# A feed-forward way down in seven products of half blocks, for sixteen of its twenty-two weight tiles

## The reference

```python
def conv_ffn(h, buf, w_up, b_up, w_dw, b_dw, w_down, b_down):
    u = h @ w_up + b_up                       # 1024 -> 5632
    xp = jnp.concatenate([buf.astype(u.dtype), u], axis=1)
    new_buf = xp[:, xp.shape[1] - (FFN_K - 1):]
    c = causal_dwconv(xp, w_dw, b_dw)         # 3 taps
    a, v = jnp.split(c, 2, axis=-1)
    return (jax.nn.silu(a) * v) @ w_down + b_down, new_buf   # 2816 -> 1024
...
        x = x + out
```

## Time and profile before

| | us |
|---|---|
| median of 3 runs (2735.18 to 2738.17) | 2737.77 |
| the profiled execution | 2733.82 |
| its span, first to last instruction | 2732.0 |
| PE busy | 2674.6 (98%) |
| DVE busy | 2121.9 (78%) |
| POOL busy | 1283.9 (47%) |
| ACT busy | 842.9 (31%) |
| mean DMA rate | 86 GB/s |

### The profile page before, as it was taken

The page is one execution under the profiler, slowest core; times in us unless marked ns, Lnnn a source line. Parts: engine busy times, 40 slices in busy tenths (PEclk is TensorE's granted clock), DMA queues, the critical chain, the costliest instruction groups (busy, mean ns, idle before and its releaser), DMA issues.

```text
span 2732.0 us, 42103 instructions
## 1 busy us (share of the span) xinstructions
PE 2674.6 (98%) x17516; PEld 2631.1 (96%) x17516; DVE 2121.9 (78%) x2447; ACT 842.9 (31%) x1267; POOL 1283.9 (47%) x928
## 2 busy tenths in 40 slices
PE   8999989999999999999999999999999999999998
PEld 8999889999999999999999999989999999999998
DVE  8998657999999855566777777797799999985555
ACT  3001624444444300021221221232444444430002
POOL 5223484777777522252212122127577777752224
PEclk9999999999999999999999999999999999999999
DMA  5222143222221432231111111115322222243222
GB/s 157 55 63 52 57 185 132 73 73 73 73 73 73 177 106 81 91 116 47 40 48 48 40 48 42 46 57 191 132 73 73 73 73 73 73 176 105 84 91 78
DMA packets 136398, 233.78 MB, mean 86 GB/s; under 512 B 67984, under 2 KB 86416, under 8 KB 136208
## 3 DMA queue, kind: packets, MB, share of 16 engines
q1 hardware_dynamic: 59120, 137.12, 14.7%
q10 hardware_dynamic: 77088, 93.97, 10.2%
HBM read 171.86 MB, written 59.20 MB: 85 GB/s over the span
## 4 chain that ended last, share of the span: by engine, by line
PE 86%; DVE 9%; POOL 3%; issue 1%; ACT 1%; DMA 0%; ACTq 0%; DVEq 0%; POOLq 0%
PE BANKS L1066 34%; PE BANKS L1026 26%; PE BANKS L1355 13%; PE BANKS L1629 3%; PE BANKS L1173 2%; PE BANKS L1411 2%; PE BANKS L1399 1%; PE BANKS L1314 1%; DVE C L2716 1%; POOL WL L828 1%; DVE XL L2302 1%; DVE HGA L2874 1%; PE BANKS L1456 1%; PE BANKS L1466 1%; DVE BANKS L2390 0%
## 5 line engine op out<-in xcount | busy, mean ns | idle before, releaser
L1066 PE MATMUL BANKS<-XB_A,OPS 128*128 128x288 f32 x3432 | 513.1, 298 | 7.9 <-ACT U L1996 7.8
L825 POOL TENSOR_TENSOR SMALL<-WRAW 128x1 f32<-128x1 f32 x108 | 26.8, 248 | 1005.4 <-PE BANKS L1026 502.2
L1066 PEld LDWEIGHTS BANKS<-XB_A,OPS 128*128 128x128 f32 x3432 | 475.1, 189 | 12.3 <-issue 10.1
L1066 PE MATMUL BANKS<-XB_B,OPS 128*128 128x288 f32 x2904 | 436.2, 295 | 0.0
L1026 PE MATMUL BANKS<-GHL,WH 128*128 128x384 f32 x2100 | 421.7, 335 | 6.3 <-POOL WL L828 3.6
L1066 PEld LDWEIGHTS BANKS<-XB_B,OPS 128*128 128x128 f32 x2904 | 403.5, 189 | 0.0
L1026 PEld LDWEIGHTS BANKS<-GHL,WH 128*128 128x128 f32 x2100 | 369.6, 188 | 7.7 <-issue 4.0
L2529 DVE TENSOR_TENSOR X<-BANKS,X 128x1152 f32<-128x1152 f32 x152 | 206.2, 1357 | 218.3 <-PE BANKS L1026 210.9
L2716 DVE SCALAR_TENSOR_TENSOR C<-U,HGA,C 128x1168 f32<-128x1168 f32 x176 | 275.8, 1587 | 40.9 <-ACT C L2015 39.4
L828 POOL TENSOR_TENSOR WL<-WRAW,WH 128x1024 fp32r<-128x1024 f32 x108 | 264.7, 2451 | 8.6
L855 POOL TENSOR_TENSOR OPS<-RAW,OPS 128x512 fp32r<-128x512 f32 x126 | 164.0, 1314 | 199.0 <-ACT OPS L1924 199.0
(11 more groups left out here) (308 smaller groups left out, 5033.3 us busy)
## 6 DMA issues: line engine op xcount, KB each, us to landing
WRAW<-in_w SPq DMA_DIRECT2D x100, 512.0 KB, 3.5
RAW<-in_w SPq DMA_DIRECT2D x84, 512.0 KB, 4.3
GR<-g_kept ACTq DMA_DIRECT2D x22, 1152.0 KB, 5.3
g_kept<-C ACTq DMA_DIRECT2D x44, 512.0 KB, 2.6
x_kept<-X ACTq DMA_DIRECT2D x24, 576.0 KB, 3.1
XB_BF<-x_kept SPq DMA_DIRECT2D x16, 576.0 KB, 8.0
ops_kept<-PRE SPq DMA_DIRECT2D x14, 512.0 KB, 2.6
OPS<-ops_kept SPq DMA_DIRECT2D x14, 512.0 KB, 3.7
```

The source lines that it names most:

```text
L1066: ins = nc.tensor.matmul(out[:, cols], w[:, a, p, :], x[:, b, cols], start=s in OPENS and p == 0 and q == 0, stop=p == PAIRS - 1 and q == ...
```

## The change

In both layers the way down keeps three groups as they are: 0, 1 and 10 (PLAIN), that is the first four and the last two weight tiles. The sixteen tiles between are taken as four quads of four tiles. A quad has two couples: a couple is the four tiles of the quad for four of the eight output tiles. It is computed in seven products of half blocks, as on the way up, for each of two pairs of output channels (ab = 0, 1), and the two pairs alternate: 14 products a couple, each 2 pairs x 3 parts x 2 pieces = 12 matmuls of 288 columns (`way_couple`). Eight couples a layer, 16 in all. "Rank" is the place of a product in its couple, 0 to 13.

- PE: product r waits for its weights (op_lo), and for DVE's read of the product four before it (read_v); each pair has two PSUM banks.
- Weights: SP loads the raw weights of a couple (four DMAs of 256 KB, rows of 1 KB) into WRAW, one buffer, after POOL's last low of the couple before. POOL makes 8 sums and 14 lows of 256 columns a couple (`way_ops`), ACT 14 highs (`way_cast`). They stand in a ring of 12 slots: four in the place of XH, eight in WH and WL. A cast waits for the product 12 before it, in couple 0 for the plain group 1.
- Inputs: SP loads the gates of a quad (eight DMAs of 288 KB) into buffers of their own for even and odd quads, each after the quad before the last. DVE makes 8 sums and 14 lows of 576 columns a quad (`way_prep`), ACT 14 highs (`way_high`), placed among the casts of the couples one ahead. DVE does one preparation of the next quad after each read from rank 5 of the first couple to rank 12 of the second, the preparations for quad 0 in groups 0 and 1, none in the last two couples.
- Output: DVE adds every product (576 columns) to half a tile of X (`way_read`), 14 a couple, in place of eight adds of 1152 a group.
- The splits of the sixteen tiles, their gates' loads on ACT's queue, high parts of 2304 columns and DVE's low parts go. The low part of group 1 goes from DVE to POOL. The last group's gates come by SP to GR_END, its low part is made by DVE in two halves in couple 7.
- The counts of the semaphores on the way up change with it (`done_no`, `read_no`, `raw_landed`), not its work. Two semaphores now serve two of the fetched parts of X each.

The core of the diff:

```diff
-FFN_UNITS = FT
-FFN_TILES = FGROUPS * KD
+PLAIN = (0, 1, FGROUPS - 1)
+QUADS = (FT - 2 * len(PLAIN)) // 4
+COUPLES = QUADS * KD // 4
+UP_ROWS = FT + 2 * COUPLES
+FFN_UNITS = 2 * len(PLAIN)
+FFN_TILES = len(PLAIN) * KD
...
+        WAY_RING = 12
...
+        WAY_PREP = (("sum", T1), ("low", B11), ("sum", NT2), ("sum", NT3), ("sum", T4), ("low", B21), ("low", NT2),
+                    ("low", T1), ("low", NT3), ("low", B22), ("low", T4))
...
+        def way_op(r):
+            slot = r % WAY_RING
+            if slot < 4:
+                v = XB_B[:, WAY_RING_AT + 512 * slot:WAY_RING_AT + 512 * (slot + 1)]
+            else:
+                of = WH if slot % 4 < 2 else WL
+                v = of[:, (slot - 4) // 4, slot % 2 * 512:(slot % 2 + 1) * 512]
+            return v.rearrange("p (h k c) -> p h k c", h=2, k=2)
...
+                def way_raw_load(n, ab):
+                    half, a = n % 2, ab * 512
+                    two = WRAW[:, ab, :].rearrange("p (a j w) -> p j a w", a=2, j=2)
+                    for j in range(2):
+                        stored = down_stored(layer, 4 * (n // 2 + 1) + 2 * j + half)
+                        sp.dma_start(two[:, j], d_w[stored, :, a:a + 512].rearrange("p (a w) -> p a w", a=2)
+                                     ).then_inc(up_raw[ab], 16)
...
+                for n in range(1, COUPLES):
+                    if n % 2:
+                        q = n // 2 + 1
+                        if q == 1:
+                            full(sp, t0 + 2 * KD - 1)
+                            sp.wait_ge(g_lo, len(PLAIN) * layer + 2)
+                        else:
+                            sp.wait_ge(up_done, way_done_no(layer, 2 * q - 3, T4, 1))
+                        if q < QUADS:
+                            for p in range(2):
+                                for s in WAY_GATE:
+                                    gate_load(q, p, s)
+                        else:
+                            sp.wait_ge(g_kept, 32 * FT * (layer + 1))
+                            sp.dma_start(GR_END[:], GKEPT[layer, FT - 2:FT].rearrange("g p t -> p g t")).then_inc(g_in, 16)
+                    sp.wait_ge(op_lo, way_op_no(layer, n - 1, T4, 1))
+                    way_raw_load(n, 0)
+                    way_raw_load(n, 1)
+                sp.wait_ge(op_lo, way_op_no(layer, COUPLES - 1, T4, 1))
+                down_load(4)
+                down_load(5)
...
+                pool.wait_ge(g_hi, layer * len(PLAIN) + 2)
+                nc.gpsimd.tensor_tensor(GHL[1][:, 1], GR[:], GHL[1][:, 0].bitcast(F32), ALU.subtract).then_inc(g_lo, 1)
+                split(u0 + 2)
+                split(u0 + 3)
+                pool.wait_ge(ffn_out, 16 * (layer + 1))
+                for n in range(COUPLES):
+                    way_ops(layer, n)
+                split(u0 + 4, used=(way_done_no(layer, COUPLES - 1, NT2, 1), up_done))
+                split(u0 + 5, used=(way_done_no(layer, COUPLES - 1, NT3, 1), up_done))
...
+                    out, a, b, how = ((0, way_raw(ab, 1, 0), way_raw(ab, 1, 1), ALU.add),
+                                      (1, way_raw(ab, 0, 0), way_tmp(ab, 0), ALU.subtract),
+                                      (0, way_raw(ab, 0, 1), way_tmp(ab, 1), ALU.add),
+                                      (1, way_raw(ab, 1, 0), way_raw(ab, 0, 0), ALU.subtract))[t]
+                    nc.gpsimd.tensor_tensor(way_tmp(ab, out), a, b, how).then_inc(op_sum, 1)
...
+                    w = way_op(way_rank(n, s, ab))
+                    pool.wait_ge(op_hi, way_op_no(layer, n, s, ab))
+                    nc.gpsimd.tensor_tensor(w[:, 1], source, w[:, 0].bitcast(F32), ALU.subtract).then_inc(op_lo, 1)
...
+                for ab in range(2):
+                    pool.wait_ge(up_raw[ab], way_raw_landed(layer, n, ab))
+                    added(ab, 0)
+                    added(ab, 1)
+                for s in (B11, B21, NT2, T1):
+                    lower(s, 0)
+                    lower(s, 1)
...
+                for ab in range(2):
+                    added(ab, 2)
+                    added(ab, 3)
+                for s in (NT3, B22, T4):
+                    lower(s, 0)
+                    lower(s, 1)
...
+                def way_couple(q, n):
+                    for s in range(PRODUCTS):
+                        for ab in range(2):
+                            pe.wait_ge(op_lo, way_op_no(layer, n, s, ab))
...
+                                pe.wait_ge(read_v, way_read_no(layer, n, s - 2, ab))
+                            w, out = way_op(way_rank(n, s, ab)), way_region(n, s, ab)
+                            for p in range(2):
+                                if n % 2 == 0 and ab == 0:
+                                    pe.wait_ge(xb_lo, way_low_no(layer, q, s, p))
+                                x = way_x(q, s, p)
+                                for k, (a, b) in enumerate(((0, 0), (0, 1), (1, 0))):
+                                    for c in range(2):
+                                        cols = slice(c * SUB, (c + 1) * SUB)
+                                        ins = nc.tensor.matmul(out[:, cols], w[:, a, p, :], x[:, b, cols],
+                                                               start=s in OPENS and p == 0 and k == 0,
+                                                               stop=p == 1 and k == 2, skip_group_check=True)
+                            ins.then_inc(up_done, 1)
...
+                def way_high(q, p, k):
+                    s = WAY_HIGHS[k]
+                    if s in (B11, B21, B22):
+                        act.wait_ge(way_in[p], 64 * (QUADS * layer + q + 1))
+                    else:
+                        act.wait_ge(xb_sum, way_sum_no(layer, q, s, p))
+                    A(way_x(q, s, p)[:, 0, :], way_whole(q, s, p), ACT.Identity).then_inc(xb_hi, 1)
+                def way_cast(n, s, ab):
+                    r = way_rank(n, s, ab)
+                    if r >= WAY_RING:
+                        act.wait_ge(up_done, way_done_no(layer, 0, 0, 0) + r - WAY_RING)
+                    elif r < 4:
+                        act.wait_ge(g_rdy, FT * (layer + 1))
+                    else:
+                        full(act, t0 + KD + (3 if r < 8 else 7))
+                    if s in (B11, B21, T4):
+                        act.wait_ge(up_raw[ab], way_raw_landed(layer, n, ab))
+                        source = way_raw(ab, 1, 1) if s == T4 else way_raw(ab, 0, s)
+                    else:
+                        t, out = {T1: (0, 0), NT2: (1, 1), B22: (2, 0), NT3: (3, 1)}[s]
+                        act.wait_ge(op_sum, way_opsum_no(layer, n, ab, t))
+                        source = way_tmp(ab, out)
+                    A(way_op(r)[:, 0], source, ACT.Copy).then_inc(op_hi, 1)
+                def way_casts(n, q, p, after):
+                    for s in range(PRODUCTS):
+                        for ab in range(2):
+                            if q < QUADS:
+                                for k in range(PRODUCTS):
+                                    if after[k] == 2 * s + ab:
+                                        way_high(q, p, k)
+                            way_cast(n, s, ab)
...
+                for k in range(PRODUCTS):
+                    way_high(0, 0, k)
+                way_casts(0, 0, 1, (0, 0, 0, 1, 2, 4, 6))
+                for n in range(1, COUPLES):
+                    q = (n + 1) // 2
+                    if n % 2:
+                        way_casts(n, q, 0, (3, 3, 4, 5, 6, 8, 10))
+                    else:
+                        way_casts(n, q, 1, (0, 0, 1, 2, 4, 6, 8))
+                gates_high(2)
...
+                def way_prep(q, p, k):
+                    what, s = WAY_PREP[k]
+                    out = way_whole(q, s, p)
+                    if what == "low":
+                        dve.wait_ge(xb_hi, way_high_no(layer, q, s, p))
+                        V.tensor_tensor(way_x(q, s, p)[:, 1, :], out, way_x(q, s, p)[:, 0, :].bitcast(F32), ALU.subtract
+                                        ).then_inc(xb_lo, 1)
+                        return
...
+                def way_read(n, s, ab):
+                    dve.wait_ge(up_done, way_done_no(layer, n, s, ab))
+                    if s in (B21, NT3, B22):
+                        dve.wait_ge(read_v, way_read_no(layer, n, {B21: B11, NT3: T1, B22: NT2}[s], ab))
+                    m = 4 * (n % 2) + 2 * ab + (s in (T1, NT3, T4))
+                    x = half(m, 0 if s in (B11, B21, T4) else 1)
+                    V.tensor_tensor(x, way_region(n, s, ab), x, ALU.add).then_inc(read_v, 1)
...
+                for n in range(COUPLES):
+                    q = n // 2 + 1
+                    for s in range(PRODUCTS):
+                        for ab in range(2):
+                            way_read(n, s, ab)
+                            at = way_rank(n % 2, s, ab)
+                            if q < QUADS:
+                                if 0 <= at - 5 < len(WAY_PREP):
```

(59 more changed lines are left out.)

184 lines of the change are left out of this document (136 added, 48 removed).

## The result

The changed kernel takes **2745.64 us** (median of ten runs, 2739.69 to 2749.53) beside 2736.09 for the kernel before (ten runs, 2734.96 to 2738.17): a ratio of 1.0033, 95% interval 1.0023 to 1.0043. It is slower by 9.6 us where 24 us less were forecast. The profiled run took 2745.89 us with a span of 2744.1, against 2733.8 and 2732.0.

A forecast was written before the change was run, and what follows sets the result against it. TensorE was taken to bound the way down. From the profiled 2733.8 us, minus 41.0 for matmuls, plus 14 for stalls and 1 for entries gave 2707.8; with 4.0 back to the median, 2712 us, range 2693 to 2735.

The forecast's parts named there:

- Part 1: Way-down matmuls: a couple takes 22.40 us, 2.56 less than a group; 16 couples in two layers save 41.0 us.
- case B: Rival, 2732 us: products of 12 matmuls cost 0.08 us each at the switch (18 us) over a stall of 17; chance 0.14.
- Part 2: GpSimd in the couples: 22 operations at 0.724 us, 15.9, plus raw load 3.8: 19.7 us a couple, 2.7 below TensorE.
- part 4: GpSimd's lead in the couples: 7.7 us at couple 1, falling 2.3 a couple; TensorE stalls 7 us a layer, 14 in all.
- Part 3: Gate preparations on VectorE beside GpSimd: blocking 0.45 us each, 5.0 for 11; a GpSimd couple 24.7 us against TensorE's 22.4.
- near 193: Sign of a right forecast: a layer's way down near 193 us for eight couples instead of 199.7.
- Part 4's own sign of failure: In the couples: the lead estimate is wrong if TensorE never waits, or waits from couple 1 on.
- Part 5: Ends of the way down: preparations and group 1's low fit into group 0; 1 us for both entries together (0 to 4).
- C: Rival, 2747 us: raw buffer's round trip, load 5 us, blocking 0.6, stalls and lower clock 56 against 41; chance 0.10.
- A: Rival, 2697 us: the cover holds in the couples, a GpSimd couple is 22.8 us, the lead lasts to the end; chance 0.28.
- the Trainium skill's rule of the whole instruction: VectorE with two SBUF inputs and GpSimd reading SBUF block each other fully; all 66 preparations paying whole length gives near 2724.

The follow-up runs named there:

- e10_entry_bare: Changed kernel with group 1's low back on VectorE and the first quad's 22 preparations writing a constant without reading: 2732.2 us, ratio 0.9990 to the kernel before.
- e9_spread: Changed kernel with group 1's low on VectorE, highs ahead of casts, T4's parts earlier, and the first quad's preparations spread over groups 0 and 1: 2699.1 us, ratio 0.9869.
- e3: Changed kernel with ScalarE making the next quad's highs ahead of the casts that wait for the raw load: 2720.6 us, ratio 0.9942 to the kernel before.
- e4: Changed kernel with T4's parts made ahead of those of NT3 and B22, so the raw load can start four GpSimd operations earlier: 2714.0 us, ratio 0.9916.

## Why the prediction was wrong

**Right.** Part 1: the pitch and the 41.0 us. Nothing stands between products of twelve, so case B's switch does not exist. Part 2: GpSimd alone takes 0.73 to 0.74 us for 256 columns against an estimate of 0.724. In the first half of a quad the stall is at the rank that part 4 names, 11; in the second half, where it names none, it is at 13.

**Part 3: the mean was right, the course was not.** GpSimd lost 145 x (0.935 - 0.729) = 29.9 us over 66 preparations between 1000 and 1170: 0.45 each, as taken. Its couples average 25.5 us against 24.7 forecast; the load is the difference, 32.6 us of waits in seven couples or 4.7 each instead of 3.8. Two things were missed. VectorE pays as well, 0.95 instead of 0.74 us for a preparation, 0.21 x 66 = 14 us a layer that the sum does not hold. And the loss is lumpy: 28 us in the couple that runs beside VectorE's dense stretch, 23 in the next. Elsewhere two numbers of the prediction are misread or slipped, and nothing rests on them: the earlier trace rows shows ScalarE busy 2.1 and GpSimd 10.7 of the 40 us, not 4 and 13, and the sum of part 4 makes eight couples 186.2 us, not the "near 193" of its signs.

**Part 4 is the step that failed.** The lead at couple 1 was to be 7.7 us. GpSimd's first low for it ended at about 1010.0 (half of a pair of 1.97 from 1009.03) and TensorE came at 1016.4: 6.4. It was to fall by 2.3 a couple, to 5.4. It fell by 5.6 (28.0 - 22.4) and more: the first low of couple 2 came at about 1038.2, and TensorE at full pitch would have come at 1038.8, a lead of 0.6. The working said itself how much lead the order wants, 4.4 us and 2.5 more in the second half of a quad, so it was gone in the first couple after the entry and not in the fourth. From there on GpSimd's whole excess is paid, 18.5 and 17.9 us in the two layers, where I had taken 7. The bound of 20 for both layers was too low as well: it let the lead shorten every layer's bill, though nearly the whole of it is needed for the order to run at all. Part 4's own sign of failure, TensorE waiting from couple 1 on, is what the trace shows.

**Part 5 failed too.** I took 1 us for both entries and 4 at most; they cost 14.6. The words "fit into the 25 us of group 0" counted GpSimd's time and not what it stands next to: the earlier trace rows had shown an operation of 1168 columns and one of GpSimd lengthen each other, and I used that row for the couples only. The preparations were added tile by tile against 3.12 us without the operations of the last way-up unit that VectorE still has to do in group 0 (one of 1168 columns and one of 1024 took 5.90 and 3.36 us beside GpSimd, 1.43 and 1.22 without). e10_entry_bare shows the two causes to be the whole of it but 0.9 us, and e9_spread that placing them otherwise is enough.

**Rivals.** C (2747 us, given one chance in ten) names the mechanism: raw round trip, meetings, lower clock. Its load of 5 us is near the 4.7, its 0.6 for a meeting is above the 0.45, and its 28 us a layer (21 of stall and 7 of clock) compare with 18 (in the window of 180 us, 9.7 and about 5). It left the entries' 14.6 out, and the two errors nearly cancel: that its 2747 is so near the measured 2745.6 is luck, though its mechanism is not. A's argument was the way up, where GpSimd works 37.3 of 50 us and TensorE loses nothing; in the couples it works 140 of 180, hardly a larger share. The meetings are there on the way up as well (L849 has a median of 1.80 us over a least of 1.29). So neither the busy share nor the meetings tell the two stages apart. In the couples it is the refill of the single raw buffer with the order behind it (e3, e4); no run tested what keeps the way up free of stalls. By the Trainium skill's rule of the whole instruction (SBUF — State Buffer, "Who interferes with whom") the prediction said 2724. That number has no working. In the prediction's own terms the rule gives a GpSimd couple of 15.9 + 3.8 + 11 x 0.75 = 28.0 us, more than C's 27.5, so C's 2747 or more. What both engines pay here for one preparation is 0.45 + 0.21 = 0.66 us of the rule's 0.75, so the rule is nearly right in size as a mean; it does not tell of the order that turns the loss into a stall.

## What to carry to other kernels

Where a producer refills a single buffer once a turn and has a few us of lead, don't spread its excess evenly over the turns: take the worst turn, and subtract from the lead what the consumers' orders need. Two engines that held each other up did no harm here once the order around them left no one waiting behind them; moving the last read of a single buffer four operations forward was worth 32 us, and moving the first quad's preparations by a few tiles 6 us by the ratios and 10 by the stages. When an operation is moved "into free time" of an engine, look up what runs beside it on the engine that it meets, not only how long it is.

## What the runs showed of the hardware

VectorE with two SBUF operands and GpSimd fall into step and stay there for eight operations of GpSimd and more, in one of two patterns: VectorE loses 0.59 us on each preparation (0.74 to 1.33) and GpSimd 0.24 on each operation (0.74 to 0.98), or VectorE loses nothing and GpSimd 0.61 (0.74 to 1.35), one operation for every add and preparation. So a preparation costs both engines together 0.59 + 2 x 0.24 = 1.07 us in the first pattern, more than its own 0.74, and 0.61 in the second; the mean of 0.66 above hides this, and some preparations meet nothing. The first pattern stood while GpSimd made the lows of four products in a row and gave way to the second where it went over to its next sums, at 1018, 1069 and 1120 us in layer 0 of the changed kernel. With reductions of the same length in the place of the preparations neither occurs. The longest single meeting in the rows read here was 4.48 us: VectorE's operation of 1168 columns, 1.42 alone, took 5.90 beside one of GpSimd of 2304 columns that takes 5.15.
